# Scan stage of a bidirectional hybrid encoder: row fetches one slot sooner, second SiLU later, copies on ScalarE, every direction sum on GpSimd

## What is computed

```python
h = rmsnorm(x, norm1_g[i])
u = h @ w_in[i]
q, k, v, z, xbc, dt_raw, sc_b, sc_c, sc_x = jnp.split(u, split_at, axis=-1)
a_out = attention_mixer(...)                     # 8 heads
s_out = ssd_mixer(z, xbc, dt_raw, ...)           # 16 heads of 64, forward + backward chunked scans, 4 chunks of 128
c_out = sc_b * dwconv(sc_c * sc_x, w3)           # short gated convolution, 512 channels
x = x + concat([a_out, s_out, c_out]) @ w_out[i]
x = x + conv_ffn(rmsnorm(x, norm2_g[i]), ...)

# ssd_mixer, for each direction (chunked scan):
decay  = exp(where(lower, a_cs[l] - a_cs[s], -inf))
y_diag = einsum(cb * decay, X)                   # inside a chunk
states = einsum(B, X * exp(a_end - a_cs))        # what a chunk hands on
y_off  = einsum(C, s_in) * exp(a_cs)             # from earlier chunks
y = (y_fwd + y_bwd + d_skip * xs) * silu(z)      # then a grouped RMSNorm
```

## Time and profile before

| what | before |
|---|---|
| median of 3 runs | 1690.19 us (1689.67 to 1690.52) |
| the profiled execution: its time | 1689.15 us |
| the profiled execution: span of the trace | 1687.4 us |
| TensorE matmul, busy | 1650.3 us, 98% |
| VectorE, busy | 994.2 us, 59% |
| ScalarE, busy | 655.1 us, 39% |
| GpSimd, busy | 679.8 us, 40% |
| granted TensorE clock, mean | 0.996 |

### The profile page before, as it was taken

One profiled execution on the slowest core, in us unless ns is written; L12 is line 12 of the kernel. 1 busy time (PEld: TensorE's weight loads), 2 busy tenths in 40 slices (PEclk: granted clock), 3 DMA queues, 4 the chain that ended last, 5 costly groups with the idle time before them and its releaser, 6 DMA issues.

```text
span 1687.4 us, 20449 instructions
## 1 busy us (share of the span) xinstructions
PE 1650.3 (98%) x7940; PEld 1309.0 (78%) x7940; DVE 994.2 (59%) x1576; ACT 655.1 (39%) x900; POOL 679.8 (40%) x339
## 2 busy tenths in 40 slices
PE   7999999999999999999999999999999999999999
PEld 5777777877778888888877777778777788888887
DVE  5589868877774545422236898687677654545100
ACT  5445552334443333332244555422343433333221
POOL 3432222233345555554443222223234455555443
PEclk9999999999999999999999999999999999999999
DMA  5532134443223232322224221344432223232233
GB/s 166 129 96 76 60 104 127 129 135 112 88 88 99 89 100 88 100 91 94 91 88 125 85 73 63 114 139 122 135 97 91 93 91 100 87 100 89 93 100 106
DMA packets 56415, 170.93 MB, mean 101 GB/s; under 512 B 5792, under 2 KB 10656, under 8 KB 56320
## 3 DMA queue, kind: packets, MB, share of 16 engines
q1 hardware_dynamic: 55936, 168.88, 32.4%
q0 software_dynamic: 384, 0.75, 0.4%
HBM read 166.24 MB, written 3.38 MB: 101 GB/s over the span
## 4 chain that ended last, share of the span: by engine, by line
PE 86%; DVE 5%; DMA 3%; issue 2%; SPq 1%; ACT 1%; POOL 1%; DVEq 0%; ACTq 0%
PE banks L1107 26%; PE banks L1109 25%; PE banks L1108 25%; DMA sb_e<-sum_rows 3%; PE banks L1197 2%; PE banks L1176 2%; PE banks L1185 2%; DVE sb_w_lo L782 1%; PE banks L1264 1%; SPq L314 1%; PE banks L1156 1%; PE banks L1277 1%; DMA sb_w_raw<-w_in 1%; PE banks L1251 1%; DVE sb_e L859 0%
## 5 line engine op out<-in xcount | busy, mean ns | idle before, releaser
L403 POOL TENSOR_TENSOR sb_w_lo<-sb_w_raw,sb_w_hi 128x1024 fp32r<-128x1024 f32 x202 | 490.8, 2430 | 632.6 <-ACT sb_w_hi L496 632.6
L1107 PE MATMUL banks<-sb_h_hi,sb_w_hi 128*128 128x512 f32 x1360 | 558.9, 411 | 20.5 <-POOL sb_w_lo L403 11.4
L1109 PE MATMUL banks<-sb_h_hi,sb_w_lo 128*128 128x512 f32 x1360 | 538.1, 396 | 0.0
L1108 PE MATMUL banks<-sb_h_lo,sb_w_hi 128*128 128x512 f32 x1360 | 537.5, 395 | 0.0
L496 ACT ACTIVATE sb_w_hi<-sb_w_raw 128x1024 fp32r<-128x1024 f32 x258 | 272.7, 1058 | 670.6 <-PE banks L1109 658.0
L1107 PEld LDWEIGHTS banks<-sb_h_hi,sb_w_hi 128*128 128x128 f32 x1360 | 256.9, 189 | 104.7 <-issue 37.4
L1108 PEld LDWEIGHTS banks<-sb_h_lo,sb_w_hi 128*128 128x128 f32 x1360 | 257.3, 189 | 61.7 <-issue 6.9
L1109 PEld LDWEIGHTS banks<-sb_h_hi,sb_w_lo 128*128 128x128 f32 x1360 | 256.7, 189 | 60.3
L1072 DVE TENSOR_TENSOR banks<-banks,sb_rstd 128x512 f32<-128x512 f32 x88 | 61.5, 699 | 144.0 <-PE banks L1109 135.7
L1109 PE MATMUL banks<-sb_ff_hi,sb_w_lo 128*128 128x512 f32 x352 | 138.9, 395 | 0.0
L1107 PE MATMUL banks<-sb_ff_hi,sb_w_hi 128*128 128x512 f32 x352 | 138.9, 395 | 0.0
(11 more groups left out here) (197 smaller groups left out, 2257.8 us busy)
## 6 DMA issues: line engine op xcount, KB each, us to landing
sb_w_raw<-w_in SPq DMA_DIRECT2D x88, 512.0 KB, 3.4
sb_w_raw<-w_up SPq DMA_DIRECT2D x88, 512.0 KB, 3.4
sb_w_raw<-w_out SPq DMA_DIRECT2D x32, 512.0 KB, 3.4
sb_w_raw<-w_down SPq DMA_DIRECT2D x32, 512.0 KB, 3.3
sb_e<-sum_rows SPq DMA_DIRECT2D x16, 512.0 KB, 6.5
sb_bias_t<-bias_rows SPq DMA_DIRECT2D x16, 448.0 KB, 6.4
sb_exp_cs<-sum_rows SPq DMA_DIRECT2D x32, 192.0 KB
sb_w_raw<-w_down SPq DMA_DIRECT2D x16, 384.0 KB, 3.0
```

The costliest lines, as they stand in the source:

```text
L403: g.tensor_tensor(WLO[:, n % 2, :], W[:, n % 2, :], WHI[:, n % 2, :].bitcast(F32), ALU.subtract).then_inc(w_lo.handle, 1)
L1107: mm(out, whi, hhi, start=start, stop=False)
L1108: mm(out, whi, hlo, start=False, stop=False)
L1109: return mm(out, wlo, hhi, start=False, stop=stop)
```

## The change

Five things, all in the scan stage of both layers. SyncE issues `head_rows(h)` one slot sooner, ahead of one more weight load. The first two state copies of each group (VectorE, L884) and the copy of the convolution's product to its high part (VectorE, L1010) become ScalarE activations with the semaphores `sin_first` and `sc_hi`. The second SiLU of a layer is issued after the weight chunk's high part of slot 20 and no more ahead of it. GpSimd adds the directions of the odd heads too, so `within` has one matmul per head and chunk and waits for both sums.

```diff
@@ sync, scalar
-                if slot - 2 in SEG_AT:
-                    head_rows(SEG_AT[slot - 2])
+                if slot - 1 in SEG_AT:
+                    head_rows(SEG_AT[slot - 1])
...
-                if s and SLOTS[s - 1] in (("z", 3), ("z", 7)):
-                    for last in (SLOTS[s - 1][1] - 1, SLOTS[s - 1][1]):
-                        b, n = TILE_BANK["z", last]
-                        act.wait_ge(*evac[b].at(n + 1))
-                    sc.activation(Z[:, :, :], Z[:, :, :], ACT.Silu).then_inc(z_done.handle, 1)
-                    sc.preload_act_table_set("natural_log_exp_and_others")
+                if s and SLOTS[s - 1] == ("z", 3):
+                    gate_silu(3)
                 high_after(kind, i)
+                if s and SLOTS[s - 1] == ("z", 7):
+                    gate_silu(7)
+                if kind == "sc" and i % 3 == 2:
+                    b, n = TILE_BANK[kind, i]
+                    act.wait_ge(*evac[b].at(n + 1))
+                    sc.activation(rm["mh_sc"][:, i // 3, :], SCP[:, :], ACT.Copy).then_inc(sc_hi.handle, 1)
...
+                for grp in range(SSD_GROUPS):
+                    if s == GROUP_AT[grp] + 1:
+                        for d in range(2):
+                            act.wait_ge(*st_mm.at(6 * grp + d + 1))
+                            sc.activation(SIN[:, d, 0, :], bank(4 + d), ACT.Copy).then_inc(sin_first.handle, 1)
@@ gpsimd
-                if s in WEIGH_AT and WEIGH_AT[s] % 2 == 0:
+                if s in WEIGH_AT:
                     add_directions(WEIGH_AT[s])
@@ vector
-            if i == 0:
-                dve.wait_ge(*st_mm.at(n + 1))
-                v.tensor_copy(SIN[:, d, 0, :], bank(4 + d)).then_inc(sin_done.handle, 1)
-                return
...
-                        for j in range(2):
+                        for j in range(2 * (s > GROUP_AT[grp] + 1)):
...
-                    dve.wait_ge(*evac[b].at(n + 1))
-                    v.tensor_copy(rm["mh_sc"][:, t, :], SCP[:, :]).then_inc(sc_hi.handle, 1)
@@ tensor: within(t)
-            pe.wait_ge(*gs_done.at(t + 1))
-            pe.wait_ge(*g_done.at(2 * t + 2))
+            pe.wait_ge(*gs_done.at(2 * t + 2))
...
-                for h, d in ((2 * t, 0), (2 * t + 1, 0), (2 * t + 1, 1)):
+                for h in (2 * t, 2 * t + 1):
                     half = 64 * (h % 2)
...
-                             head_e(h)[:, d, P * c:P * c + P], start=d == 0, stop=d == h % 2)
+                             head_e(h)[:, 0, P * c:P * c + P], start=True, stop=True)
```

More of the change, by code:

```diff
@@ L268, in build_trunk @@
     tok_tr, tok_copied = sem("tok_tr", 10), sem("tok_copied", 10)
-    cb_mm, cb_done, xs_done, st_mm, sin_done = sem("cb_mm", 2), sem("cb_done", 4), sem("xs_done", 12), sem("st_mm", 12), sem("sin_done", 12)
-    seg_done, e_done, g_done, y_mm = (
-        sem(n, SSD_HEADS) for n in ("seg_done", "e_done", "g_done", "y_mm"))
-    gs_done = sem("gs_done", SSD_HEADS // 2)
+    sin_first = sem("sin_first", 4)
+    cb_mm, cb_done, xs_done, st_mm, sin_done = sem("cb_mm", 2), sem("cb_done", 4), sem("xs_done", 12), sem("st_mm", 12), sem("sin_done", 8)
+    seg_done, e_done, g_done, gs_done, y_mm = (
+        sem(n, SSD_HEADS) for n in ("seg_done", "e_done", "g_done", "gs_done", "y_mm"))
     yo_mm, y_read, t_read, z_copied, y_comb = (sem(n, 8) for n in ("yo_mm", "y_read", "t_read", "z_copied", "y_comb"))
@@ L566, in at_evac, with gate_silu @@
             sc.activation(PTS[:, u % 4, :, :], bank(4 + u % 2).rearrange("p (j i) -> p j i", i=P), ACT.Copy).then_inc(at_ptc.handle, 1)
+        def gate_silu(last):
+            for i in (last - 1, last):
+                b, n = TILE_BANK["z", i]
+                act.wait_ge(*evac[b].at(n + 1))
+            sc.activation(Z[:, :, :], Z[:, :, :], ACT.Silu).then_inc(z_done.handle, 1)
+            sc.preload_act_table_set("natural_log_exp_and_others")
         def at_out(t):
@@ L646, in _ @@
                     sc.activation(head_e(h), head_e(h), ACT.Exp).then_inc(e_done.handle, 1)
-                if s and SLOTS[s - 1] in (("z", 3), ("z", 7)):
-                    for last in (SLOTS[s - 1][1] - 1, SLOTS[s - 1][1]):
-                        b, n = TILE_BANK["z", last]
-                        act.wait_ge(*evac[b].at(n + 1))
-                    sc.activation(Z[:, :, :], Z[:, :, :], ACT.Silu).then_inc(z_done.handle, 1)
-                    sc.preload_act_table_set("natural_log_exp_and_others")
-                high_after(kind, i)
+                if s and SLOTS[s - 1] == ("z", 3):
+                    gate_silu(3)
+                high_after(kind, i)
+                if s and SLOTS[s - 1] == ("z", 7):
+                    gate_silu(7)
+                if kind == "sc" and i % 3 == 2:
+                    b, n = TILE_BANK[kind, i]
+                    act.wait_ge(*evac[b].at(n + 1))
+                    sc.activation(rm["mh_sc"][:, i // 3, :], SCP[:, :], ACT.Copy).then_inc(sc_hi.handle, 1)
                 if s == 0:
@@ L881, in state_in @@
             (d, c), i = direction_chunk(j), j // 2
-            if i == 0:
-                dve.wait_ge(*st_mm.at(n + 1))
-                v.tensor_copy(SIN[:, d, 0, :], bank(4 + d)).then_inc(sin_done.handle, 1)
-                return
             dve.wait_ge(*(t_read.at(4) if grp else rows_stored.at(32)))
             col = 64 + column(d, 8 * grp)
-            dve.wait_ge(*sin_done.at(n - 1))
+            dve.wait_ge(*(sin_first.at(2 * grp + j - 1) if j < 4 else sin_done.at(4 * grp + j - 3)))
             step(v.tensor_tensor(T[:, d, :].rearrange("p (h e) -> p h e", e=64), SIN[:, d, i - 1, :].rearrange("p (h e) -> p h e", e=64),
@@ L1249, in chunk_state @@
             if j >= 2:
-                pe.wait_ge(*sin_done.at(n - 1))
+                pe.wait_ge(*(sin_first.at(2 * grp + j - 1) if j < 4 else sin_done.at(4 * grp + j - 3)))
             mm(bank(4 + d), BT[:, c, :], SQ[:, j % 2, :], start=True, stop=True).then_inc(st_mm.handle, 1)
         def within(t):
-            pe.wait_ge(*gs_done.at(t + 1))
-            pe.wait_ge(*g_done.at(2 * t + 2))
+            pe.wait_ge(*gs_done.at(2 * t + 2))
             if t % 4 == 0:
@@ L1261, in within @@
             for c in range(QT):
-                for h, d in ((2 * t, 0), (2 * t + 1, 0), (2 * t + 1, 1)):
+                for h in (2 * t, 2 * t + 1):
                     half = 64 * (h % 2)
                     ins = mm(BANK[half:half + 64, 6 + t % 2, P * c:P * c + P], XT[:, c, 64 * (h % 8):64 * (h % 8) + 64],
-                             head_e(h)[:, d, P * c:P * c + P], start=d == 0, stop=d == h % 2)
-                    if c == QT - 1 and d == h % 2:
+                             head_e(h)[:, 0, P * c:P * c + P], start=True, stop=True)
+                    if c == QT - 1:
                         ins.then_inc(y_mm.handle, 1)
@@ L1270, in from_states @@
             grp, at = t // 4, slice(P * (t % 4), P * (t % 4) + P)
-            pe.wait_ge(*sin_done.at(6 * grp + 6))
+            pe.wait_ge(*sin_first.at(2 * grp + 2))
+            pe.wait_ge(*sin_done.at(4 * grp + 4))
             if t:
```

## The result

| | before | after |
|---|---|---|
| median, runs beside each other on one chip | 1689.67 us (1688.38 to 1691.08, 11 runs) | 1694.90 us (1692.02 to 1697.92, 11 runs) |
| profiled execution: time, span | 1689.15, 1687.4 us | 1695.72, 1693.9 us |
| VectorE, ScalarE, GpSimd busy | 994.2, 655.1, 679.8 us | 1003.5, 664.8, 715.5 us |
| granted TensorE clock, mean | 0.996 | 0.991 |

The ratio of after to before is 1.0030, 95% interval 1.0020 to 1.0039: slower by 5 us. The forecast was 1691.5 with a range of 1679 to 1699. The time lies in the range, but the range is 20 us wide and reaches from 11 us faster to 9 us slower, so that alone says little. The forecast had 1.3 us on top of the 1690.19 of before, and 5.2 came. Of the three outcomes it had given "slower" the smallest chance, 0.30.

A forecast was written before the change was run, and what follows sets the result against it. TensorE, 98% busy, was taken as the bound, with waits at slots 10 and 21 through VectorE's late rows. Terms -2.6 - 3.7 + 8.0 = +1.7 us on 1689.15 gave 1690.9, stated as 1691.5; range 1679 to 1699.

The forecast's parts named there:

- What bounds the kernel: TensorE, 98% busy, waits at slots 10 and 21 through VectorE's late rows; 19.8 us over both layers.
- Fewer matmuls: At within, eight matmuls instead of twelve: 1.02 us instead of 1.90, 16 times 0.88, 14 us of TensorE's work.
- Rows one slot sooner: Before seg, all VectorE waits for rows vanish; load(10) lands at about 287.3, its high part waits 1.2 us.
- Copies: Product casts leaving VectorE give about 3 us; state copies fall into waiting time, and ScalarE takes them for nothing.
- Odd heads on GpSimd: Sums end 2.3 us after weigh; TensorE waits 2.8, 3.5, 3.9 us at within(0), (3), (7) in layer 0.
- The second SiLU: Slot 20's low part starts near 382.4, but scan_low(0) blocks VectorE until 388.0; seg(14) gains 2.65 us, not 7.
- clock term: Lower clock behind the waits: 1.9 us each at within(3) and within(7), 0.2 at within(0); 4.0 us per layer.
- The sum: Whole kernel: -2.6 - 3.7 + 8.0 = +1.7 us on the profiled 1689.15, so 1690.9; given as 1691.5.
- B: Rival: the same waits at within but shorter, near 2.5 us, where the clock held; 1681 to 1685 us; chance 0.27.
- C: Rival: GpSimd's sums stay hidden, waits at within under 1 us; 1656 to 1670 us; chance 0.08.
- D: Rival: slot 10's weight chunk lands late, at 288.4 or after, delaying VectorE's chain; 1696.5 us; chance 0.22.
- A: The forecast case: waits move to GpSimd's sums, clock falls behind two per layer; 1688 to 1696 us; chance 0.38.

The follow-up runs named there:

- e3: The kernel before with only the rows of each head asked for one slot sooner: 1677.8 us, ratio to before 0.9921.
- e1: The changed kernel without GpSimd's sums for the odd heads, so within has twelve matmuls again: 1676.8 us, ratio to before 0.9917.
- e8: The kernel before with only the later second SiLU and ScalarE's state and product copies: 1688.1 us, ratio to before 0.9992.
- e5: The changed kernel without odd heads' sums, and with scan_low(0) to (3) one slot later each: 1670.8 us, ratio to before 0.9888.
- e6: The changed kernel with the odd heads' sums on VectorE right behind weigh, not on GpSimd: 1680.9 us, ratio to before 0.9950.
- e10: The changed kernel with three filling matmuls in front of within(3) and within(7): 1689.0 us, ratio to before 0.9998.

## Why the prediction was right or wrong

- **What bounds the kernel**: right. Both waits came through VectorE from rows that were late, and e3, which touches nothing else, is worth 13.8 us, where the two waits had been counted at 19.8.
- **Fewer matmuls**: right, `within` takes 1.02 us where the clock is whole (rows of within(0) above), and 16 times 0.88 is 14 us of work. e1 against after shows that nothing of it arrived.
- **Rows one slot sooner**: right. VectorE waits for no rows any more, in either layer, where it waited 24.6 us in all. load(10) landed 14.6 us after its issue at 272.86, at 287.5 (forecast 287.3). VectorE's wait for its high part was 0.40 us in layer 0 and 1.80 in layer 1, forecast 1.2.
- **Copies**: no run shows a cost, and none shows the 3 us. Together with the SiLU's move they gave 1.0 us with the rows in time (e1 against e3) and nothing that can be told with the rows late (e8).
- **Odd heads on GpSimd**: right in place and size: 2.72, 3.40 and 3.91 us in layer 0 for 2.8, 3.5 and 3.9. 13 of the 16 sums of layer 0 took 2.2 to 2.3 us, as the even ones did; those of heads 4, 7 and 9 came first and took 1.3. Not foreseen: waits of 1.1 us at within(5) and of 1.5 us for a low part at tile 23, both ahead of the longer wait at within(7), and head 9's sum, whose turn pushes GpSimd's gates into slot 16, so that the low part there takes 1.99 us and tile 18 waits 0.74 us for z. What it costs was not tried.
- **The second SiLU**: the mechanism was right, the block only moved to scan_low(0). The times were 3.5 us later than forecast: the low part of slot 20 at 385.91 for 382.4, scan_low(0) at 391.50 for 388.0. 3.1 of the 3.5 were lost before group 1, since tile 14 starts 3.3 us later than in before, where the forecast without the clock had 0.2; 2.1 of them the forecast had itself, in the clock term. e5 shows that the block itself was the thing to remove.
- **The sum**: the total was too small. On the profiled executions it had +1.7 us, and +6.6 were measured (+5.2 by the medians, so 1.4 of what follows belongs to this pair of executions). Layer 0 was to give +1.4 and gave +3.9. Of these 2.5 us, 0.6 and 0.9 are the **clock term** at within(3) and within(7): they cost 2.5 and 2.8 us and not 1.9 each, because the forecast had taken 1.9 from tiles behind a wait, and the shortened `within` itself also runs at the low clock (1.91 for 1.02). Another 0.7 us is within(3) starting at 316.88 instead of 316.2, less the 0.2 that the clock term had for within(0). Of the 0.7, 0.35 is VectorE's low part of slot 8, which came at 288.64 behind load(10), where the forecast's terms give 288.3. 0.5 us are open.
- **The clock behind within(0)** fell in layer 0 (tiles 7 and 8 took 12.79 us, 11.27 before) and not in layer 1 (11.24). The forecast had 0.2 us for it since load(10) hides it, and that was right: VectorE's low part of slot 8 starts 18.44 us behind within(0) in layer 0 and 18.39 in layer 1. VectorE spent the 1.5 us waiting for tile 7 in one layer and for load(10) in the other.
- **Layer 1** was to give +0.3 and gave +2.6. The forecast had counted as a reserve that its chain was 1.1 us longer in before (139.84 us from within(0) to within(7), 138.74 in layer 0). In after it is again 1.1 us longer (139.36 and 138.25), but for another reason. VectorE was level with layer 0: weigh(7) starts 41.80 us behind within(0), in layer 0 41.94. Then head 7's sum came behind VectorE's low part and took a turn more:

```profile
1153.67 2.25 POOL L433 TENSOR_TENSOR sb_squares<-sb_squares 128x512 f32<-128x512 f32 x1
...
1153.21 1.59 DVE L796 TENSOR_TENSOR sb_w_lo<-sb_w_raw,sb_w_hi 128x1024 fp32r<-128x1024 f32 x1 [0.62 <-ACT sb_w_hi L495]
```

  In layer 0 this sum took 1.25 us, and the forecast had 1.1 for it. The turn is 1.0 of the 2.3 us. The clock adds 0.3 (2.8 and 1.3 us at within(3) and within(7), forecast 1.9 each). It also fell at within(2), for 1.5 us, which was not expected, but within(3) behind it waits 2.72 us for the sum, so that this did not reach the end. About 1 us is left: the same 0.5 in front of within(3) as in layer 0, and 0.5 that is open there too.
- **Rivals**: B needed waits near 2.5 us; they came out at 2.7 to 3.9. C did not occur; even e6, with the odd sums on VectorE, is at 1680.9, outside its 1656 to 1670. D did not occur: load(10) landed at 287.5, before the 288.4 from which it decides, and equally far behind within(0) in layer 1 (17.3 us), and TensorE has no wait at slot 10. A held, with its waits at the forecast places and its time at the slow end.

The Trainium skill's rule that was weighed ("SBUF — State Buffer", section Who interferes with whom) agrees with the traces: the sum of head 7 took 1.25 us in layer 0 of after, where it came first, and 2.24 in e10, where it came second.

## What to carry to other kernels

Work taken off the bounding engine only counts if the instructions that replace it end before that engine would have started: here 14 us of matmuls went, and a sum of 1.3 to 2.3 us at the end of VectorE's chain turned them into a loss of 18 us against the same kernel without the sums. When a stall is removed, find the next tie on the same engine first; the kernels that are best here leave out all or most of these sums and move the low parts `scan_low` that blocked VectorE. A wait that appears in front of the bounding engine must be priced with what follows it at the lower clock, the short product too: 9.4 us here at four places, behind 14 us of waits. With these waits filled, three of the places kept the high clock, which brought back 5 to 6.

## What the runs showed of the hardware

- Two engines on SBUF operands take turns by order of arrival: 0.54 us of difference in the arrival of VectorE's low part moved 1.0 us from one engine to the other (1.25 and 2.23 us against 2.24 and 1.56).
- At within(3) of layer 0 the granted clock fell to 1.2 GHz while TensorE stood still, 2 to 3 us into the wait (0.80 in 315 to 316, 0.50 from 316 on), so the first matmuls behind the wait of 3.4 us were slow already. At within(0) of layer 0 it fell only when TensorE was working again (start at 270.20; 1.00 in 270 to 271, 0.62 in 271 to 272).
- Behind waits of 2.72 us it fell twice (within(0) of layer 0, within(3) of layer 1), behind 2.73 us at within(0) of layer 1 it did not, and behind 1.94 us at within(2) of layer 1 it fell. The length of the wait alone does not say whether it falls.
- A filling matmul of 512 columns in the scan's own operand form took 0.87 us and one of a weight tile 0.23.
- Behind the two transfers of `pair_exps(1)` the DMA engines of after are nearly idle while a weight chunk of 512 KB waits to land. The window says 0.13 of 16 engines, which is as much as two busy ones, at 51 GB/s:

```profile
277.00:278.00 1.00, 1.00 (x6) 0.78 (x6) 0.00 (x0) 0.76 (x1) 0.00 (x0) 1.00 0.13 51
```

The Trainium skill ("DMA: Bandwidth & Descriptors", section Why a DMA increments its semaphore by 16 and not by 1) states that a transfer runs on the largest number of engines, at most 16, that divides the slowest dimension of both its access patterns. Here these are the two rows of a pair and the 128 partitions of the buffer, and the trace agrees with two engines. Another order of the dimensions was not tried.
